# Two reorderings and a bf16 routing map in a two-layer mixture-of-experts encoder step

## The reference

```python
s = jax.nn.sigmoid((t @ w_router).astype(jnp.float32))
sel = s + b_router.astype(jnp.float32)
grp_score = lax.top_k(sel.reshape(-1, N_GROUPS, EXPERTS_PER_GROUP), TOP_K)[0].sum(-1)
grp = jnp.argmax(grp_score, axis=-1)
in_grp = (jnp.arange(N_EXPERTS) // EXPERTS_PER_GROUP)[None, :] == grp[:, None]
_, idx = lax.top_k(jnp.where(in_grp, sel, -jnp.inf), TOP_K)
w = jnp.take_along_axis(s, idx, axis=-1)
w = w / jnp.sum(w, axis=-1, keepdims=True)
gates = jnp.sum(jax.nn.one_hot(idx, N_EXPERTS, dtype=jnp.float32) * w[..., None], axis=1)
a = jax.nn.silu(jnp.einsum('nd,edf->nef', t, w_gate)) * jnp.einsum('nd,edf->nef', t, w_up)
a = a * gates[:, :, None].astype(a.dtype)
return jnp.einsum('nef,efd->nd', a, w_down).reshape(B, T, D)
```

## Time and profile before

| | |
|---|---|
| median of 3 runs | 1601.84 us (1598.27 to 1605.42) |
| the profiled execution | 1610.96 us, span 1609.2 us |
| busy, share of the span | PE 87%, PEld 71%, DVE 65%, ACT 54%, POOL 28% |
| mean granted TensorE clock | 0.926 of full speed |
| chain that ended last, by engine | PE 68%, DVE 12%, issue 7%, DMA 5%, ACT 5% |

### The profile page before, as it was taken

One profiled execution on the slowest core, in us unless ns is written; L12 is line 12 of the kernel. 1 busy time (PEld: TensorE's weight loads), 2 busy tenths in 40 slices (PEclk: granted clock), 3 DMA queues, 4 the chain that ended last, 5 costly groups with the idle time before them and its releaser, 6 DMA issues.

```text
span 1609.2 us, 27667 instructions
## 1 busy us (share of the span) xinstructions
PE 1400.7 (87%) x10165; PEld 1139.7 (71%) x10165; DVE 1040.8 (65%) x1445; ACT 866.2 (54%) x1545; POOL 457.6 (28%) x362
## 2 busy tenths in 40 slices
PE   5899999988749999999928999999794699999990
PEld 3688887757537777888828888887573577788870
DVE  1756642236458989889966444443555499898885
ACT  3344455462218777888733444443512377788872
POOL 1111121110025656666510000000000366566650
PEclk9799999989859999999968999999796699999995
DMA  9465633242328989999962643343505399999984
GB/s 313 118 214 182 207 114 113 76 170 80 148 86 314 355 332 347 371 374 385 377 200 61 176 148 114 113 124 114 184 18 212 120 334 353 340 359 365 372 322 185
DMA packets 167822, 357.59 MB, mean 222 GB/s; under 512 B 20770, under 2 KB 82978, under 8 KB 159026
## 3 DMA queue, kind: packets, MB, share of 16 engines
q1 hardware_dynamic: 155380, 331.94, 58.3%
q0 software_dynamic: 12352, 24.40, 4.3%
HBM read 340.56 MB, written 33.54 MB: 232 GB/s over the span
## 4 chain that ended last, share of the span: by engine, by line
PE 68%; DVE 12%; issue 7%; DMA 5%; ACT 5%; SPq 1%; DVEq 1%; ACTq 0%; POOL 0%; POOLq 0%
PE bank L609 16%; PE bank L611 15%; PE bank L610 15%; DVE ring_r L2108 4%; PE bank L320 3%; DMA ring<-in_w_down 2%; ACT work_r L2101 2%; PE bank L695 2%; PE bank L1550 2%; PE bank L1588 1%; PE bank L762 1%; PE bank L2400 1%; PE bank L1565 1%; DMA ring<-in_w_ada 1%; PE bank L1015 1%
## 5 line engine op out<-in xcount | busy, mean ns | idle before, releaser
L610 PE MATMUL bank<-ring_r,arena_r 128*128 128x512 f32 x816 | 322.3, 395 | 0.0
L2108 DVE TENSOR_TENSOR ring_r<-ring,work_r 128x1024 fp32r<-128x1024 f32 x102 | 182.4, 1814 | 20.7 <-ACT work_r L2101 20.7
L609 PE MATMUL bank<-ring_r,hT_r 128*128 128x384 f32 x512 | 185.5, 362 | 0.0
L2108 DVE TENSOR_TENSOR ring_r<-ring,arena_r 128x1024 fp32r<-128x1024 f32 x96 | 156.3, 1661 | 34.6 <-ACT arena_r L2101 34.5
L610 PEld LDWEIGHTS bank<-ring_r,arena_r 128*128 128x128 f32 x816 | 155.8, 191 | 30.5
L611 PE MATMUL bank<-ring_r,work_r 128*128 128x384 f32 x512 | 172.7, 337 | 0.0
L610 PE MATMUL bank<-ring_r,hT_r 128*128 128x384 f32 x512 | 172.3, 337 | 0.0
L2108 DVE TENSOR_TENSOR ring_r<-ring,hT_r 128x1024 fp32r<-128x1024 f32 x108 | 151.5, 1430 | 21.6 <-ACT hT_r L2101 20.7
L2101 ACT ACTIVATE hT_r<-ring 128x1024 fp32r<-128x1024 f32 x144 | 146.9, 1055 | 19.5 <-DMA ring<-in_w_gate 16.1
L2101 ACT ACTIVATE arena_r<-ring 128x1024 fp32r<-128x1024 f32 x128 | 127.6, 1052 | 35.6 <-DMA ring<-in_w_down 35.5
L2101 ACT ACTIVATE work_r<-ring 128x1024 fp32r<-128x1024 f32 x136 | 137.6, 1060 | 3.0 <-DMA ring<-in_w_up 2.7
(11 more groups left out here) (359 smaller groups left out, 2910.1 us busy)
## 6 DMA issues: line engine op xcount, KB each, us to landing
ring<-in_w_gate SPq DMA_DIRECT2D x136, 512.0 KB, 6.4
ring<-in_w_up SPq DMA_DIRECT2D x136, 512.0 KB, 6.2
ring<-in_w_down SPq DMA_DIRECT2D x68, 1024.0 KB, 8.0
bc<-in_w_ada SPq DMA_DIRECT2D x40, 1024.0 KB, 7.4
bc<-in_w_in_even SPq DMA_DIRECT2D x64, 192.0 KB, 5.6
bc<-in_w_in_odd SPq DMA_DIRECT2D x64, 192.0 KB, 3.6
arena<-moe_out SPq DMA_DIRECT2D x8, 1024.0 KB
ring<-in_w_ada SPq DMA_DIRECT2D x3, 2048.0 KB, 13.6
```

The lines of the kernel that those rows point to most:

```text
L609: nc.tensor.matmul(acc, rows_hi, w_hi, start=first, stop=False)
L610: nc.tensor.matmul(acc, rows_hi, w_lo, start=False, stop=False)
L2108: dve.tensor_tensor(r32(piece(m_low[v], q)), piece(m_low[v], q), f32(piece(m_high[v], q)), ALU.subtract).then_inc(MO[f"lo_{c}"], 1)
```

## The change

1. **Out projection, PE.** `turn(j)` moves behind the first half of tile j + 2, and the logits of tile j behind the second half of tile j + 2, but for the last tiles: the turn of the fourth in order and the logits of the third come behind the last product. ACT rounds two pieces of the up weights before it copies out the last tile.
2. **Weights.** SP loads up, then gate, writes the rows to `moe_in`, then loads down.
3. **Routing map.** `slot_hot` and `item_val` become bf16. The row number is two integers (`tile_no`, `row_in`) that are exact in bf16, the gate three bf16 parts. POOL makes the three gate parts once the near table stands; a second set of 20 products (75 columns, bank 3) sums them, and DVE adds the three sums at the end of the routing. DVE drops three copies out of PSUM and a memset, and adds one addition.
4. **First gather.** It reads its column straight from `slot_tok`, with no copy to `now_tok`.
5. **Remainders.** DVE's up 0 goes ahead of the routing chain, gate 0 between the tables and the wait for the map, gate 2 and 3 behind the barrier. ACT rounds gate 0 and 1 before the sigmoid's Exp, and loads the Silu table ahead of the barrier.
6. **Expert loop, DVE.** `product(n)` moves ahead of gate 0 and `rows_low` of the next item.

The diff, without its unchanged lines and 8 columns of indent:

```diff
@@ -110,7 +110,9 @@
+arena_at = -(-nc.sbuf_base // 32) * 32
...
+rt_b = nc.alloc_sbuf_tensor_at("rt_b", [P, 2 * 1440], BF16, offset=arena_at + 4 * 10240)
@@ -585,7 +587,7 @@
-RT = sems("rt", "logits", "part", "e", "turned", "self", "mask", "pos", "cnt", "near", "far", "map", "slots", "h")
+RT = sems("rt", "logits", "part", "e", "turned", "self", "mask", "pos", "cnt", "near", "far", "map", "split", "slots", "h")
@@ -1955,12 +1957,15 @@
-    for j in range(1, TILES):
-        if j >= 2:
-            out_product(pe, l, j, 0, OUT_KS[l])
+    out_product(pe, l, 1, 1, OUT_KS[l])
+    for j in range(2, TILES):
+        out_product(pe, l, j, 0, OUT_KS[l])
+        turn(j - 2)
+        out_product(pe, l, j, 1, OUT_KS[l])
+        if j < TILES - 1:
...
-        out_product(pe, l, j, 1, OUT_KS[l])
-        turn(j - 1)
+    turn(TILES - 2)
+    router_logits(pe, name, TILES - 3)
@@ -1995,6 +2000,7 @@
+    split_high(act, "u", layer_first(act, l), 0, 1)
@@ -2115,11 +2121,14 @@
-slot_hot = rt2[:, 0:1280].rearrange("p (n s) -> p n s", s=P)
-item_ge = rt2[:, 1280:1540].rearrange("p (n i) -> p n i", i=MAX_ITEMS + 1)
-item_hot = rt2[:, 1540:1790].rearrange("p (n i) -> p n i", i=MAX_ITEMS)
-item_val = rt2[:, 1790:2290].rearrange("p (n i) -> p n i", i=2 * MAX_ITEMS)
-row_no, item_0, slot_no = rt2[:, 2290:2300], rt2[:, 2300:2326], rt2[:, 2326:2454]
+slot_hot = rt_b[:, 0:1280].rearrange("p (n s) -> p n s", s=P)
+item_hot = rt_b[:, 1280:1530].rearrange("p (n i) -> p n i", i=MAX_ITEMS)
+item_val = rt_b[:, 1536:1536 + 50 * MAX_ITEMS].rearrange("p (n i) -> p n i", i=5 * MAX_ITEMS)
+gate_part = [rt_b[:, 2800 + 10 * i:2810 + 10 * i] for i in range(3)]
+gate_rest = rt2[:, 1440:1450]
+item_ge = rt2[:, 1536:1796].rearrange("p (n i) -> p n i", i=MAX_ITEMS + 1)
+tile_no, row_in = rt2[:, 2290:2300], rt2[:, 2559:2560]
+item_0, slot_no = rt2[:, 2300:2326], rt2[:, 2326:2454]
@@ -2147,21 +2156,27 @@
-            last = nc.tensor.matmul(bank[2][:, 0:2 * MAX_ITEMS], slot_hot[0:r, ct, :], item_val[0:r, ct, :],
+            last = nc.tensor.matmul(bank[2][:, 0:2 * MAX_ITEMS], slot_hot[0:r, ct, :], item_val[0:r, ct, 0:2 * MAX_ITEMS],
...
+    pe.wait_ge(s["split"], 7 * (l + 1))
+    for ct in range(2 * TILES):
+        r = rows(ct % TILES)
+        last = nc.tensor.matmul(bank[3][:, 0:3 * MAX_ITEMS], slot_hot[0:r, ct, :], item_val[0:r, ct, 2 * MAX_ITEMS:],
+                                start=ct == 0, stop=ct == 2 * TILES - 1)
+    last.then_inc(s["map"], 1)
...
+    first = layer_first(act, l)
+    split_high(act, "g", first, 0, 1)
...
-
-    first = layer_first(act, l)
-    split_high(act, "g", first, 0, 1, 2, 3)
-    split_high(act, "u", first, 0, 1)
+    split_high(act, "g", first, 2, 3)
+    act.preload_act_table(ACT.Silu)
@@ -2173,18 +2188,38 @@
-    pool.iota(row_no.rearrange("p (c t) -> p c t", c=2), pattern=[[TOK, 2], [P, TILES]], base=1, channel_multiplier=1,
+    pool.iota(tile_no.rearrange("p (c t) -> p c t", c=2), pattern=[[TOK, 2], [P, TILES]], base=0, channel_multiplier=0,
...
+    pool.iota(row_in, pattern=[[0, 1]], base=1, channel_multiplier=1, allow_small_or_imprecise_dtypes=True)
...
+    pool.memset(rv(13), 0.0)
...
+
+    lk = Link(pool, s["split"], base=7 * l)
+    flat = gates[:, :, :].rearrange("p c t -> p (c t)")
+    pool.wait_ge(s["near"], l + 1)
+    lk.do(pool.tensor_copy(gate_part[0], flat))
+    lk.do(pool.tensor_tensor(gate_rest, flat, gate_part[0], ALU.subtract))
+    lk.do(pool.tensor_copy(gate_part[1], gate_rest))
+    lk.do(pool.tensor_tensor(gate_part[2], gate_rest, gate_part[1], ALU.subtract))
+    for k in range(3):
+        lk.step(pool.tensor_tensor(item_val[:, :, (2 + k) * MAX_ITEMS:(3 + k) * MAX_ITEMS], item_hot,
+                                   gate_part[k].unsqueeze(2).to_broadcast([P, 2 * TILES, MAX_ITEMS]), ALU.mult))
...
-    item_rows_in(pool, layer_first(pool, l), 0)
+    first_rows_in(pool)
...
+
+def first_rows_in(pool):
+
+    settle(pool)
+    pool.indirect_dma_start(m_x, None, moe_in, bass.IndirectOffsetOnAxis(slot_tok[:, 0:1], 0),
+                            bounds_check=TOK - 1, oob_is_err=False).then_inc(MO["x"], 16)
+    pool.sem_inc(MO["now_tok"], 1)
@@ -2222,6 +2257,8 @@
+    first = layer_first(dve, l)
+    split_low(dve, "u", first, 0)
@@ -2266,8 +2303,8 @@
-    cnt, nt_, end, st = rt[:, 2144:2160], rt[:, 2160:2176], rt[:, 2176:2192], rt[:, 2192:2208]
-    lk.do(dve.tensor_copy(cnt, bank[1][:, TILES * NE:(TILES + 1) * NE]))
+    nt_, end, st = rt[:, 2160:2176], rt[:, 2176:2192], rt[:, 2192:2208]
+    cnt = bank[1][:, TILES * NE:(TILES + 1) * NE]
@@ -2276,10 +2313,9 @@
-    lk.do(dve.tensor_copy(dst[:, 0:NT * NE], bank[1][:, 0:NT * NE]))
-    lk.do(dve.memset(dst[:, NT * NE:TILES * NE], 0.0))
-    lk.do(dve.tensor_copy(dst[0:DEC, NT * NE:TILES * NE], bank[1][0:DEC, NT * NE:TILES * NE]))
-    lk.do(dve.tensor_tensor(T3(dst, NE), T3(dst, NE), bt(st, NE), ALU.add))
+    lk.step(dve.tensor_tensor(T3(dst[:, 0:NT * NE], NE), T3(bank[1][:, 0:NT * NE], NE),
+                              st.unsqueeze(1).to_broadcast([P, NT, NE]), ALU.add))
+    lk.do(dve.tensor_tensor(dst[0:DEC, NT * NE:TILES * NE], bank[1][0:DEC, NT * NE:TILES * NE], st[0:DEC, :], ALU.add))
@@ -2289,15 +2325,15 @@
-    lk.step(dve.tensor_tensor(item_val[:, :, 0:MAX_ITEMS], item_hot, wide(row_no, MAX_ITEMS), ALU.mult))
-    lk.do(dve.tensor_tensor(item_val[:, :, MAX_ITEMS:2 * MAX_ITEMS], item_hot,
-                            wide(gates[:, :, :].rearrange("p c t -> p (c t)"), MAX_ITEMS), ALU.mult))
+    lk.step(dve.tensor_scalar(item_val[:, :, MAX_ITEMS:2 * MAX_ITEMS], item_hot, row_in, None, ALU.mult))
+    lk.do(dve.tensor_tensor(item_val[:, :, 0:MAX_ITEMS], item_hot, wide(tile_no, MAX_ITEMS), ALU.mult))
...
-    dve.wait_ge(s["map"], l + 1)
-    lk.step(dve.tensor_copy(slot_gate[:, :], bank[2][:, MAX_ITEMS:2 * MAX_ITEMS]))
+    split_low(dve, "g", first, 0)
+    dve.wait_ge(s["map"], 2 * l + 1)
...
+    lk.do(dve.tensor_tensor(row_of, bank[2][:, MAX_ITEMS:2 * MAX_ITEMS], row_of, ALU.add))
@@ -2319,10 +2355,11 @@
+    dve.wait_ge(s["map"], 2 * l + 2)
+    lk.do(dve.tensor_copy(slot_gate[:, :], bank[3][:, 2 * MAX_ITEMS:3 * MAX_ITEMS]))
+    lk.do(dve.tensor_tensor(slot_gate[:, :], bank[3][:, MAX_ITEMS:2 * MAX_ITEMS], slot_gate[:, :], ALU.add))
+    lk.do(dve.tensor_tensor(slot_gate[:, :], bank[3][:, 0:MAX_ITEMS], slot_gate[:, :], ALU.add))
...
-    first = layer_first(dve, l)
-    split_low(dve, "g", first, 0, 2, 3)
-    split_low(dve, "u", first, 0)
@@ -2340,12 +2377,13 @@
-    for c in "gud":
-        load(c, 0)
+    load("u", 0)
+    load("g", 0)
...
+    load("d", 0)
@@ -2463,7 +2501,6 @@
-    act.preload_act_table(ACT.Silu)
@@ -2537,6 +2574,8 @@
+    split("g", first, 2, 3)
+
@@ -2563,9 +2602,9 @@
+        product(n)
...
-        product(n)
```

## The result

The changed kernel takes 1614.6 us in the median of 20 runs (1600.4 to 1624.8), the kernel before 1605.4 in as many. The ratio is 1.0055 (95% interval 1.0032 to 1.0078): 9 us slower, where 1571 was forecast. The profiled execution took 1615.63 us.

What follows compares the result with a forecast made beforehand. PE's waits were taken as the bound: for DVE's rows in the out projection, the routing's barrier, and DVE in slow loop items. 7.2 + 4.8 + 12.8 + 6 = 30.8 us off 1601.84 gave 1571 us, range 1560 to 1585.

Steps and rivals of the forecast that it cites:

- The turns behind a half product: Out projection: PE's wait and the half clock behind it go; 7.2 us gained in layer 0, 4.8 in layer 1.
- DVE's chain ahead of the tables: Routing: four operations become two, one copy goes and a multiply becomes bf16; 0.75 us gained.
- The map and the gather: Routing: with bf16 products and no copy, `slot_tok` comes 3.8 us earlier and the gather starts between 457.6 and 459.5.
- The barrier: End of routing: barrier at 459.9 to 461.2, PE starting at 462.3, 6.4 us earlier per layer, 12.8 in both.
- `product` ahead of gate 0: Expert loop, DVE: PE's gate product follows at once in slow items; 6 us gained, bounds -5 and 12.
- POOL goes first: Rival, expert loop: POOL's gate piece takes the lock in every item, gate 0 is always slow; 1637 us, chance 0.05.
- the sign for it: Expert loop: the forecast is wrong if gate 0's remainder takes 3.4 us in more than the six items.
- DMA takes back half of the loop's gain: Expert loop: the DMA engines take back about half of what `product` ahead gains, 6 us taken of at most 12.

## Why the prediction was wrong

**The turns behind a half product: right.** 7.2 and 4.8 us were forecast, 7.0 and 5.0 came, in the changed kernel and alone. In layer 0 the wait (4.63) is most of it and the half clock behind it 1.9 us; now the clock there is 1.00.

**DVE's chain ahead of the tables: the chain right, its start not.** From its first operation to the first table it takes 13.29 us for 14.20, 0.91 less for the 0.75 forecast. But it starts 14.04 and 14.47 us behind the last product, for 13.55 in both layers before. ACT's two early roundings, put at 0 with 1 us as the other bound, are not the reason: they cost nothing, ACT's next copy comes 7.68 us behind the last product in both kernels. The sum has no term for the rounding of gate 0 and 1 that the change puts ahead of the sigmoid's Exp. ACT is at it, waiting for the second piece too, until 435.5, and the Exp starts 13.68 and 14.10 us behind the last product for 13.14. The cost is 0.5 and 0.9 us.

```profile
433.25 1.06 ACT L2107 ACTIVATE hT_r<-ring 128x1024 fp32r<-128x1024 f32 x1 [0.76 <-DMA ring<-in_w_gate]
...
435.43 0.21 ACT L2176 ACTIVATE arena<-bank 128x64 f32<-128x64 f32 x1
```

**The map and the gather: right.** From the chain's start `slot_tok` comes 3.76 us earlier (3.8). The gather starts 33.0 us behind the last product in layer 0, within the two bounds (32.0 to 33.8), and 33.4 in layer 1. The three gate parts of POOL and the four small ones take 4.6 us for 3.0.

**The barrier: the sum left out what ends it and what stands behind it.** The first transposes came 5.6 and 4.9 us earlier for 6.4. The sum lets the barrier go with DVE, at 459.9 to 461.2, and PE start 1 us behind it "or with the landed rows". But POOL's part of the barrier ends only when the gathered rows have landed (458.2 for 458.1, 1256.5 for 1256.4; in the kernel before 465.6 for 465.5, where DVE came last), and PE starts 1.0 and 1.5 us behind that, while DVE waits 2.51 and 3.83 us. The larger part of the miss lies behind the barrier. The sentence that failed there is that gate 2 and 3 on DVE "run beside PE's transposes and ACT's copy (3.4 us from PE's start to its first product), so at nothing". It priced them at 2.4 us, their time alone. POOL's first gate piece is released by the same barrier and runs between them, they took 4.52, and `rows_low` stands behind them: 2.4 and 2.2 us given back. The routing is worth 5.9 us in the trace, not 12.8.

**`product` ahead of gate 0: the step that turned the sign.** +6 was taken between -5 and 12; alone it costs 24 us, undone in the changed kernel it gives back 26.5. The prediction had the right mechanism among its rivals, *POOL goes first*, and gave it 0.05. Its price was too high, 20.6 us an item for 19.2, and the chance far too low. The step that failed is the condition, that it "decides where POOL is ready within 0.6 us behind the last down remainder". The 0.6 us are the step from `product` to the operation behind it, so the sentence says: POOL goes first only where its row starts ahead of the moved gate 0. POOL's 1.02 us behind gate 0 become 0.42 by that, and 0.42 us were taken for a win of DVE's. The distance was right, 0.42 to 0.45 us in 24 of the 32 items. The outcome was not: POOL went first in 19 of the 24. And the sign for it was written down: gate 0 at 3.4 us in more than six items.

The trace of before could not tell. It has DVE first in four items with POOL 0.04 to 0.58 us behind gate 0, but POOL had been idle ahead of its piece in all of them; straight from its gather it had cases at -0.1 us, with POOL first, and from 0.99 us on, with DVE first. What lay between was open, and that deserved far more than 0.05.

The Trainium skill, "SBUF — State Buffer", section "SBUF: two separate sides", says that of a DVE operation with two SBUF inputs and a POOL operation that reads SBUF the one that starts first has the shared ports for the whole instruction. The prediction named the exclusion and followed its consequence into the rival. The runs agree with the exclusion (and the run with `rows_low` ahead of gate 0, whose 1.27 us stayed 1.27). They do not let one read "starts first" off the rows of a profile. Of the two subtractions gate 0 starts 0.42 us ahead and is served behind. If POOL's gather counts, which starts 0.75 us ahead of gate 0, the turn is POOL's by the rule; but in the fast items of before the gather starts 0.15 us ahead of gate 0 as well, and gate 0 takes its 1.21 us (581.71 in the earlier trace rows). The measurement decides.

```profile
581.55 1.15 POOL L2194 DMA_INDIRECT arena<-moe_in,now_tok  x1 [0.87 <-ACT hT_r L2101]
```

**DMA takes back half of the loop's gain: not separated.** Once POOL waits, the DMA engines are at 1.00 of the loop and PE at 99%, and `product` ahead is worth about 4 us for the 6 forecast, which is within the scatter; what it would be with DMA to spare no run shows.
